# Twelve jobs of weights' sums in the opening stage, the other 36 thinner over attention, none in retention

## What is computed

```python
xn = rms_norm(x, norm_mix_w)
rq, rk, rv, rg, cq, ckv, kpe, ga, gb = split_columns(xn @ w_in)
q = (rms_norm(cq, q_norm_w) @ w_uq)            # 8 heads, 128 + 64 rotary
ckv = rms_norm(ckv, kv_norm_w);  kpe = rope(kpe, pos)
ret_y, mla_y, new_state = mixer_core(rq, rk, rv, q, ckv, kpe, w_ukv)
ret_branch = (head_group_norm(ret_y, ret_gn_w) * silu(rg)) @ w_ret_o
mla_branch = mla_y @ w_mla_o
merged = sigmoid(ga) * ret_branch + sigmoid(gb) * mla_branch
h = x + merged @ w_out
g, u = split(rms_norm(h, norm_ffn_w) @ w_gate_up)
h = h + (silu(g) * u) @ w_down                 # then a final rms_norm
```

## Time and profile before

| | before |
|---|---|
| median of 3 runs | 2094.2 us (2093.69 to 2095.24) |
| the profiled execution's own time | 2092.21 us |
| its span | 2090.2 us |
| TensorE busy | 1996.8 us, 96% of the span |
| VectorE, ScalarE, GpSimd busy | 1299.3, 778.0, 618.4 us |
| DMA | 348.24 MB, mean 167 GB/s |

### The profile page before, as it was taken

One profiled execution on the slowest core, in us unless ns is written; L12 is line 12 of the kernel. 1 busy time (PEld: TensorE's weight loads), 2 busy tenths in 40 slices (PEclk: granted clock), 3 DMA queues, 4 the chain that ended last, 5 costly groups with the idle time before them and its releaser, 6 DMA issues.

```text
span 2090.2 us, 35246 instructions
## 1 busy us (share of the span) xinstructions
PE 1996.8 (96%) x14160; PEld 1926.2 (92%) x14160; DVE 1299.3 (62%) x2055; ACT 778.0 (37%) x1353; POOL 618.4 (30%) x581
## 2 busy tenths in 40 slices
PE   8989899998989899999999989999999999999997
PEld 8968788787989898999999989999999999999997
DVE  6567776865455555887767796655555555432257
ACT  5334444442233225555443335544344444210010
POOL 0134434422145341150000250664444444200000
PEclk9989999999999999999999999999999999999999
DMA  8335455464256447777785732122323232663412
GB/s 308 121 103 173 155 163 165 140 235 171 76 194 216 166 159 261 277 260 278 249 296 210 256 126 97 64 104 95 115 94 115 93 116 87 251 252 111 174 54 86
DMA packets 171425, 348.24 MB, mean 167 GB/s; under 512 B 14976, under 2 KB 81472, under 8 KB 163968
## 3 DMA queue, kind: packets, MB, share of 16 engines
q1 hardware_dynamic: 171264, 345.99, 47.7%
HBM read 234.22 MB, written 111.72 MB: 166 GB/s over the span
## 4 chain that ended last, share of the span: by engine, by line
PE 79%; DVE 10%; POOL 3%; DMA 3%; issue 3%; ACT 2%; SPq 1%; DVEq 0%; ACTq 0%; POOLq 0%
PE ps L1228 24%; PE ps L1230 24%; PE ps L1229 24%; DVE tmp L2217 1%; PE ps L1329 1%; PE ps L1421 1%; PE ps L1323 1%; DVE p_exp L2452 1%; DVE negmax L2444 1%; DVE qr L2210 1%; PE ps L1484 1%; PE ps L1480 1%; PE ps L1481 1%; DMA yd<-y_spill 1%; DVE pt_lo L2210 1%
## 5 line engine op out<-in xcount | busy, mean ns | idle before, releaser
L1228 PE MATMUL ps<-s_hi,t_hi 128*128 128x272 f32 x1344 | 389.1, 290 | 9.5 <-DVE s_lo L2210 9.5
L1230 PE MATMUL ps<-s_lo,t_hi 128*128 128x272 f32 x1344 | 390.8, 291 | 0.0
L1229 PE MATMUL ps<-s_hi,t_lo 128*128 128x272 f32 x1344 | 390.0, 290 | 0.0
L1228 PE MATMUL ps<-sx_hi,t_hi 128*128 128x272 f32 x1232 | 356.8, 290 | 2.2 <-ACT u L2066 2.2
L1229 PE MATMUL ps<-sx_hi,t_lo 128*128 128x272 f32 x1232 | 356.6, 289 | 0.0
L1228 PEld LDWEIGHTS ps<-s_hi,t_hi 128*128 128x128 f32 x1344 | 256.1, 191 | 10.4 <-DVE s_lo L2210 5.9
L1230 PE MATMUL ps<-sx_lo,t_hi 128*128 128x272 f32 x880 | 255.9, 291 | 0.0
L1230 PEld LDWEIGHTS ps<-s_lo,t_hi 128*128 128x128 f32 x1344 | 255.5, 190 | 0.0
L1229 PEld LDWEIGHTS ps<-s_hi,t_lo 128*128 128x128 f32 x1344 | 255.3, 190 | 0.0
L1228 PEld LDWEIGHTS ps<-sx_hi,t_hi 128*128 128x128 f32 x1232 | 234.6, 190 | 2.5 <-DVE t_lo L2210 2.4
L1229 PEld LDWEIGHTS ps<-sx_hi,t_lo 128*128 128x128 f32 x1232 | 234.2, 190 | 0.0
(11 more groups left out here) (285 smaller groups left out, 5061.4 us busy)
## 6 DMA issues: line engine op xcount, KB each, us to landing
job<-in_weights SPq DMA_DIRECT2D x96, 256.0 KB, 3.7
t_sums<-job SPq DMA_DIRECT2D x48, 512.0 KB, 3.6
t_row<-t_sums SPq DMA_DIRECT2D x48, 512.0 KB, 7.4
y_spill<-hg_r SPq DMA_DIRECT2D x44, 544.0 KB, 3.4
yd<-y_spill SPq DMA_DIRECT2D x22, 1088.0 KB, 5.6
s_raw<-s_x SPq DMA_DIRECT2D x21, 1088.0 KB, 5.6
t_row<-in_weights SPq DMA_DIRECT2D x36, 512.0 KB, 6.6
w_stage<-in_weights SPq DMA_DIRECT2D x35, 512.0 KB, 3.9
```

The lines of the kernel that those rows point to most:

```text
L1228: nc.tensor.matmul(out, wh, xh, start=start, stop=False, skip_group_check=onto)
L1229: nc.tensor.matmul(out, wl, xh, start=False, stop=False, skip_group_check=onto)
L1230: return nc.tensor.matmul(out, wh, xl, start=False, stop=stop, skip_group_check=onto)
```

## The change

Twelve jobs, 0 to 11, are done in the opening in four groups of three. They have six tiles of their own (`early_tile`), in the places of the shared key's split form, of the new part of `ckn`, and of `xt`'s third and fourth tile, which become `cqn_hi`. A group's six loads are issued together, and its loads wait for the landing of the stores two groups before. SP's queue takes loads and stores between the spills and the items. GpSimd makes the sums of jobs 0 to 5 ahead of power 1, and those of jobs 6 to 11 behind it, ahead of shared key 0. ScalarE waits for the landing of the stores before it writes the third part of cqn and before the shared key's split; VectorE before it writes `ckn`.

The other 36 jobs are placed over attention, four in each seven tiles, and none is left for retention: there the loads, sums and stores of jobs are gone, and `x_inv` is loaded ahead of it. The load of the item `LAST_JOB_ITEM` (the second of retention) is moved from head 7's first projection behind the last loads of `xn_lo`.

```diff
-ATTENTION_JOBS = 44
+OPENING_JOBS = 12
 def job_place(job):
-    return (job % 2, job // 2) if job < ATTENTION_JOBS else (1, job - ATTENTION_JOBS // 2)
+    return job % 2, (job - OPENING_JOBS) // 2
 def job_turns():
...
+    loads, stores = {}, {}
+    for i, job in enumerate(range(OPENING_JOBS, JOBS)):
+        first = 7 * (i // 4)
+        loads[divmod(first + (0, 1, 3, 5)[i % 4], 9)] = job
+        stores[divmod(first + (2, 4, 6, 7)[i % 4], 9)] = job
+    return loads, stores
...
+        early_tile = [region("early0", 32, [4, 2 * P]), region("early1", 32, [4, 2 * P], extra=4096),
+                      region("early2", 8, [4, 2 * P]), region("early3", 8, [4, 2 * P], extra=4 * KEYS),
+                      region("early4", 2, [4, 2 * P]), region("early5", 3, [4, 2 * P])]
...
+            def early_load(group):
+                if group >= 2:
+                    sp.wait_ge(early_out[group % 2], 48)
+                elif group:
+                    sp.wait_ge(squared, 4)
+                for job in range(3 * group, 3 * group + 3):
+                    for tile in range(2):
+                        sp.dma_start(early_tile[job % 6][:, 2 * tile:2 * tile + 2, :].rearrange("p h (k c) -> p h k c", c=P),
+                                     job_source(job, tile)).then_inc(early_in[group % 2], 16)
+            def early_store(group):
+                for job in range(3 * group, 3 * group + 3):
+                    sp.wait_ge(job_sum, 4 * job + 4)
+                    sp.dma_start(job_target(job), early_tile[job % 6][:, :, :]).then_inc(early_out[group % 2], 16)
...
+            early_load(0)
+            spill((0, 1))
+            items(4, 5)
+            spill((2, 3))
+            early_load(1)
+            early_store(0)
+            items(5, 6)
+            early_load(2)
+            spill((4, 5))
+            early_store(1)
+            items(6, 7)
+            early_load(3)
+            spill((6, 7))
+            early_store(2)
+            items(7, 8)
+            early_store(3)
             items(8, I_MLA + 2)
...
-                if what == "M" and (kind, g) == ("K", 0):
+                if what == "M" and (kind, g) == ("K", 0) and h + 1 < MH:
...
                             sp.dma_start(xn_lo[:, t, :].bitcast(F32), xn_spill[:, 1, t, :]).then_inc(x_in[t], 16)
+                        items(LAST_JOB_ITEM, LAST_JOB_ITEM + 1)
...
+            sp.wait_ge(job_out[1], JOBS_END)
+            sp.dma_start(x_inv[:, :], x_inv_spill).then_inc(consts_in, 16)
...
                     if s[0] == "B":
                         turn, at_turn = divmod(9 * h + s[1], 4)
-                        late_job = ATTENTION_JOBS + turn
-                        if at_turn == 0 and turn and late_job <= JOBS:
-                            job_store(late_job - 1)
-                        if at_turn == 1 and late_job < JOBS:
-                            job_load(late_job)
-                        if at_turn == 1 and late_job == JOBS:
-                            sp.wait_ge(job_out[1], JOBS_END[1])
-                            sp.dma_start(x_inv[:, :], x_inv_spill).then_inc(consts_in, 16)
...
                         t = CQ_AT[j]
+                        if t == 2 and g == 0:
+                            act.wait_ge(early_out[1], EARLY_END)
...
+                act.wait_ge(early_out[0], EARLY_END)
...
+                if t == 0:
+                    for group in range(2):
+                        dve.wait_ge(early_out[group], EARLY_END)
...
+            for job in range(6):
+                job_sums(job)
+            power(1, x_col)
+            for job in range(6, OPENING_JOBS):
+                job_sums(job)
+            shared_key(0)
+            shared_key(1)
+            power(2, c_col)
+            shared_key(2)
+            power(3, c_col)
...
-                        if n % 4 == 3 and ATTENTION_JOBS + n // 4 < JOBS:
-                            job_sums(ATTENTION_JOBS + n // 4)
```

More of the change, by code:

```diff
@@ L493, in build @@
         piece_in = [sem(f"piece_in{i}") for i in range(8)]
-        job_in, job_out = piece_in[0:2], piece_in[2:4]
-        JOBS_END = [16 * sum(job_place(job)[0] == b for job in range(JOBS)) for b in range(2)]
-        PIECE_BASE = [2 * JOBS_END[0], 2 * JOBS_END[1], *JOBS_END, 0, 0, 0, 0]
+        job_in, job_out, early_in, early_out = piece_in[0:2], piece_in[2:4], piece_in[4:6], piece_in[6:8]
+        JOBS_END, EARLY_END = 8 * (JOBS - OPENING_JOBS), 8 * OPENING_JOBS
+        PIECE_BASE = [2 * JOBS_END] * 2 + [JOBS_END] * 2 + [2 * EARLY_END] * 2 + [EARLY_END] * 2
         c_scaled = sem("c_scaled")
@@ L831, in _, with job_source @@
             sp.dma_start(ckn[:, :, TOK:KEYS], a["cache_ckv"]).then_inc(cache_ckv_in, 16)
[L832 to L837, removed]
+            def job_source(job, tile):
+                o, p, half = job // 8, job // 2 % 4, job % 2
+                first, step = OCTET_ITEMS[o]
+                return W[first + step * (p + 4 * tile)].rearrange("p (h k) c -> p h k c", h=2)[:, :, 2 * half:2 * half + 2, :]
@@ L2836, in shared_key, with job_sums @@
                                         ALU.mult).then_inc(rot_sum, 1)
+            def job_sums(job):
+                if job < OPENING_JOBS:
+                    tile, group = early_tile[job % 6], job // 3
+                    pool.wait_ge(early_in[group % 2], 96 * (group // 2) + 96)
+                else:
+                    b, turn = job_place(job)
+                    tile = job_tile[b]
+                    pool.wait_ge(job_in[b], 32 * turn + 32)
+                b11, b21, b12, b22 = [tile[:, i, :] for i in range(4)]
+                nc.gpsimd.tensor_tensor(b22, b22, b12, ALU.subtract).then_inc(job_sum, 1)
+                pool.wait_ge(job_sum, 4 * job + 1)
+                nc.gpsimd.tensor_tensor(b12, b12, b11, ALU.subtract).then_inc(job_sum, 1)
+                pool.wait_ge(job_sum, 4 * job + 2)
+                nc.gpsimd.tensor_tensor(b11, b22, b11, ALU.add).then_inc(job_sum, 1)
+                pool.wait_ge(job_sum, 4 * job + 3)
+                nc.gpsimd.tensor_tensor(b21, b21, b11, ALU.subtract).then_inc(job_sum, 1)
+            for job in range(6):
+                job_sums(job)
             power(1, x_col)
+            for job in range(6, OPENING_JOBS):
+                job_sums(job)
             shared_key(0)
@@ L2855, in _ @@
                 fill("M", 0, "R", g)
[L2856 to L2871 removed]
+            job_loads = job_turns()[0]
             sums_at = {divmod(9 * h + at + 1, 9): job for (h, at), job in job_loads.items()}
```

58 lines of the change are left out of this document (16 added, 42 removed).

## The result

The changed kernel takes 2100.0 us (median of ten executions; nine lie between 2097.3 and 2103.2), the kernel before 2093.8 us in the same series (2090.1 to 2095.2). One execution of the changed kernel took 8709.6 us, for a reason that nothing here shows, and it is left out of the ratio (without it the median is 2099.7). That ratio is 1.0034, with a 95% interval of 1.0025 to 1.0043. The changed kernel is slower by 6 us, by more than the 0.2% that can be told from no change. The forecast was 2092.6 us and no change that can be told.

A forecast was written before the change was run, and what follows sets the result against it. TensorE was taken to bound the kernel, working 1996.8 of 2090.2 us. Opening +14.6, retention -15.2 and attention -1 gave -1.6 us: 2092.6 us on the median's scale, range 2081 to 2105.

The forecast's parts named there:

- The failing step: Opening, SP's queue: group 3's loads wait for group 1's stores, landed 66.1, start at 67.5 and land at 72.8 us.
- The clock's part: Opening: a half-clock window after TensorE's idle near 88 us, priced at 2.7 us, the mean of retention's two.
- the first 4.9 us: Opening: VectorE can build the first diagonal from 56.7 and not 51.80 us, 4.9 us late.
- the 11.9: Opening: TensorE's product with the second diagonal comes at 93.3 instead of 81.36 us, 11.9 us late.
- TensorE's idle shrinks from 6.1 to 1.4: Retention, first long wait: the weight lands 4.7 us earlier without a job's store before it, so TensorE idles 1.4 us.
- after so short an idle I take the clock not to fall: Retention, behind both shortened idles: no half clock, winning 3.3 us at the first place and 2.1 at the second.
- The -1 us: Attention: 36 jobs instead of 44 hinder VectorE's p_exp less, -1 us, bounds -4 and +2.
- Retention gives little back: Slower rival: short idles still bring half clock or prep loads queue; about 6 of 15.2 us left, 2103 us; chance 0.29.
- Opening nearly free: Faster rival: loads land some 5 us sooner or GpSimd overlaps better; opening costs +5, no clock window, 2083 us; chance 0.31.
- the HBM limit: Slower rival: HBM binds at about 358 GB/s; opening costs 17.4 us, retention gains 14, 2096.6 us; chance 0.04.
- the 1 to 5 that the prediction allowed: Opening: jobs beside VectorE's first diagonal operations can add 1 to 5 us to the first stall, disappearing in the second.

The follow-up runs named there:

- the kernel of 2076.8 us: The changed kernel with six jobs in the opening, 42 in attention, and the weights of retention issued sooner: 2076.8 us, ratio 0.9919 against the kernel before.

## Why the prediction was wrong

The forecast was that gain and loss cancel. On the traces the sum missed by 12.2 us: 4.1 in the opening, 3.5 in attention, 4.2 in retention, 0.4 in the last stage. On the medians it missed by 7.4. Neither of the two signs that were to show it wrong came (a shared key before 78 us, idles of retention above 4 us); what failed are sizes and one step on the clock.

**The opening, mechanism right, one term too small.** The order of events was the one foretold: power at 56.44 (54.9 was said), first idle near 53, shared key at 86.92 (82.7), TensorE's product at 97.6 (93.3), a stretch at half clock behind each. The failing step is "stores of group 1 to 65.4, landed 66.1; loads of group 3 start at 67.5, to 72.1, landed 72.8". SP could issue those loads only at 68.96, 6 us after the last of the stores, and they landed at 77.5, 8.5 us from issue where the step gives 6.7. The round trip through memory, which the sum built from 1.4 us to start and 0.7 to land (a split of some 2.1 us that no row shows), is 4.7 us longer than that: 2.9 because the stores' landing let SP go on at 68.96 and not at 66.1, and 1.8 in the loads themselves. Beside these loads ran the spills that SP issued right behind them, from 72.88; how much of the 1.8 us is theirs is not shown. The 4.2 us by which the shared key is later than foretold, and the 4.3 us of the product, are this, less 0.5 that the sums took less than was put. The clock's part held: 18.7 us at the token sums less 16.2 at the product leaves 2.5, where 2.7 was put. And the first 4.9 us were rightly counted as contained in the 11.9; the run with the first power sooner shows that.

What the text priced at nothing, "the new waits of ScalarE and VectorE for the last early stores (landed by 88.5) end before the late chain does", is true of the changed kernel, though they landed 4.7 us later than that (ScalarE goes on at 93.18, the product comes at 97.6), but only because the diagonal is so late: the run with both diagonals early shows that wait as the next bound, behind which a better order of GpSimd's wins 5.6 us of 18.7.

**Retention, direction right, size too large.** The first place came as foretold: "TensorE's idle shrinks from 6.1 to 1.4" was 1.5, and the clock did not fall, together -8 us. At the second, 6.8 to 1.7 was 6.8 to 2.5: the weight took 4.4 us to land, where the step has 3.6 (issued at 671.2, landed at 674.8). And "after so short an idle I take the clock not to fall" failed in this profile: 30 starts in 6.4 us, at the full pace of 7.9 per us, is 2.6 us lost where 2.1 should have been won. That step was a guess, with no row of an idle of that length behind it.

But this failure is one of this execution. Three of the other kernels have the very order of the changed kernel in retention: the one with the first power sooner, the one with both diagonals sooner and the one without jobs in the opening. Their stage takes 298.1, 298.3 and 298.1 us, 13.3 to 13.5 less than before and not 11.0. In all three TensorE stands for 2.5 us at the second place and then goes on at full clock; with the first power sooner it stands until 693.94, and the whole stretch around it reads:

```profile
691.30:699.80 8.50, 5.95 (x46) 5.58 (x46) 6.08 (x9) 1.62 (x5) 2.44 (x3) 1.00 0.24 76
```

Only with both diagonals sooner did the lower level come elsewhere in the stage, behind the 2.1 us at the first place (clock 0.60 from 611.6 to 615.9). So of the 4.2 us that retention missed by, 2.4 are the clock of this one profile, and 1.8 are what the step was really too large by; 0.8 of these are the second idle, the rest is below what single profiles can tell. At the second place the lower level followed in two of six profiles with an idle of 2.3 to 2.6 us (the changed kernel and the one with six jobs). Such an idle is to be priced at a part of what a stretch at the lower clock costs, with both ends kept for the range.

**Attention, below what a profile can tell.** The -1 us can be neither confirmed nor refuted: the stage takes 378.9 to 382.9 us in all runs but the one with 48 jobs. The three with exactly the changed kernel's attention stage have 378.9 to 380.9 (the two with GpSimd's order changed in the opening, and the one with the weights of retention sooner), the changed kernel 381.9. The kernel before has 379.4, and with its weights of retention issued sooner, which leaves attention as it is, 382.7. So two profiles of one order differ by as much as the 3.5 us that the table shows as missed.

**The rivals.** "Retention gives little back" had one thing of two right, that a short idle can still bring the half clock, at one place of two and in this profile. Its 2103 us came near the 2100.0 by luck: it took 6 us as given back, where the stage gave 11, and 14.6 us as the opening's cost, where it was 18.7, and these two errors cancel in large part. "Opening nearly free" was wrong for twelve jobs, and right for six. For the HBM limit of the Trainium skill ("DMA: Bandwidth & Descriptors", Where 436 GB/s comes from), the window from 59.1 to 65.5 has 407 GB/s between memory and SBUF at a share of 1.03: the trace again differs from the page's 358. By that figure alone the opening would have cost 17.4, near the 18.7, but not by its mechanism: what was late is a chain of waits for landings, with SP standing from 64.3 to 68.96 and GpSimd for the 8.58 us before 77.53.

Why the kernel became slower is therefore settled: the opening cost more than retention gave back, and by one longer round trip more than was put. What stays open is which of the two, GpSimd's order or the tiles' second use, would bound nine or ten jobs, and what of the landing's length is due to the transfers beside it; neither was tried.

## What to carry to other kernels

Work that is put into a free stretch of an engine is free only if it ends before that engine's next critical operation is due, and if no buffer is needed a second time: then each round costs load, sum, store and a landing, and the round trips add up. Before work is moved away from a stall, look at what stands in line behind it: here the weight loads, issued two or three units (products of one group of columns) sooner in SP's order, gave 12 us with the jobs left in place, while taking the jobs away gave 8, and putting twelve of them into the opening lost 19. Several stalls in a row on one engine are not a sum, the last one pays for all; but take it away, and the earlier one is paid in full (7.3 us). And a stage's difference between two single profiles can hold 2.4 us that are only the granted clock of one of them: look at the same stage in other kernels that leave it as it is.

## What the runs showed of the hardware

The granted clock behind a short idle is not fixed by its length, nor by what the other engines do in it. All twelve kernels end retention with the same idle of 2.50 us for st_f, and the other engines are busy for the same times in it. In six of the twelve profiles the lower level of 1.2 GHz is granted for most or all of the 2.5 us behind it (0.50 to 0.62), in the other six hardly at all (0.88 to 1.00). Idle and the stretch behind, first in the changed kernel, then in the changed kernel with the weights of retention sooner:

```profile
799.45:801.95 2.50, 0.00 (x2) 0.03 (x1) 2.47 (x7) 0.62 (x2) 1.43 (x2) 1.00 0.33 105
801.95:804.45 2.50, 2.50 (x6) 0.92 (x6) 0.06 (x1) 0.82 (x2) 0.00 (x0) 0.62 0.85 238
792.19:794.69 2.50, 0.01 (x1) 0.03 (x1) 2.47 (x7) 0.63 (x2) 1.43 (x2) 1.00 0.33 105
794.69:797.19 2.50, 2.32 (x8) 0.85 (x8) 0.71 (x3) 1.27 (x2) 0.00 (x0) 0.88 0.82 215
```

The same holds for the second place of retention: after 2.5 us (694.8 to 697.3) the engine ran at the lower level for most of 6.4 us, after 2.3 us in the kernel with six jobs for most of 4.6 us, and after 2.5 us in four other kernels not at all. Behind the idles of 5.6 us and more that are shown here the lower level followed each time. This may be part of the 5 us by which executions of one kernel differ; that is not shown.

GpSimd's sum or difference of 128x256 takes 0.72 to 0.78 us in most places of the changed kernel's opening and 1.60 to 1.79 in four: at 50.81, where VectorE's w_lo (two inputs from SBUF) had begun at 50.77 for 1.23 us, it took 1.78. The Trainium skill ("SBUF — State Buffer", SBUF: two separate sides) has the later of two such operations wait for the whole of the other. The trace agrees: 1.23 us of waiting leave about 0.6 for the operation itself, a little less than its usual 0.74. VectorE's nine diagonal operations took 2.79 us at 58.38, with GpSimd's sums beside their end, and 1.85 before: 0.9 us more, just below the 1 to 5 that the prediction allowed. Where the sums stood beside all nine, in the kernel of 2076.8 us, they took 4.25 us at 52.42; with the power behind all six jobs, so that no sums stood beside them, 1.85 again (59.41).
